# Two decoder layers on one core: half of the state products moved to the mixer's norm, the gate's 16 columns computed in fp32, the last norm done by tokens

## The reference

```python
def rms_norm(x, g):
    return x * lax.rsqrt(jnp.mean(x * x, axis=-1, keepdims=True) + EPS) * g

def half_ffn(x, g_pre, g_post, w_gate, w_up, w_down):      # D=1024, F=2816
    h = rms_norm(x, g_pre)
    f = (jax.nn.silu(h @ w_gate) * (h @ w_up)) @ w_down
    return x + 0.5 * rms_norm(f, g_post)

def mixer(h, ...):
    z = h @ w_in            # gq gk gv gg | glr: 16 columns | sq sk sv | conv
    log_a = log_sigmoid(glr @ gla_w_a2 + gla_b_a) / GLA_TAU
    # gated linear attention: per head, S_new = exp(b_last) * S + (k * exp(b_last - b))^T v
    # stick-breaking attention over 2048 cached positions, causal conv of 31 taps
    return concat(groups) @ w_out, k_new, v_new, s_new, buf_new

def decoder_layer(x, ...):
    x = half_ffn(x, ...)                                   # FFN 1
    x = x + rms_norm(mixer(rms_norm(x, mix_norm_pre)), mix_norm_post)
    return half_ffn(x, ...)                                # FFN 2
```

## Time and profile before

| | |
|---|---|
| runs of the kernel (median of 3; lowest, highest) | 1443.51 us; 1441.48, 1445.41 |
| the profiled execution | 1444.73 us, of which the trace's span is 1443.1 us |
| PE busy | 1405.8 us (97%) |
| DVE, ACT, POOL busy | 899.5 us (62%), 738.4 us (51%), 179.6 us (12%) |
| HBM read and written | 242.91 MB, 5.53 MB |
| mean granted TensorE clock | 0.99 of full speed |

### The profile page before, as it was taken

How to read it: one execution, slowest core, us unless ns; L and a number is a source line. 1 busy time by engine, 2 the same in 40 slices (tenths; PEclk the granted TensorE clock), 3 DMA queues, 4 the chain that set the end, 5 groups by cost and what they waited for, 6 DMA issues and landing times.

```text
span 1443.1 us, 26817 instructions
## 1 busy us (share of the span) xinstructions
PE 1405.8 (97%) x10515; PEld 1329.7 (92%) x10515; DVE 899.5 (62%) x1496; ACT 738.4 (51%) x1198; POOL 179.6 (12%) x326
## 2 busy tenths in 40 slices
PE   7999999999999999999999999999999999999997
PEld 6999999988877899999999999999887689999996
DVE  5665633679985766653367655355899747766542
ACT  4544433588855544343364444355886555443431
POOL 0020000323254000000000000021423510000000
PEclk9999999999999999999999999999999999999998
DMA  9565555567798575545545555556867894554441
GB/s 239 147 204 150 145 150 156 163 199 223 212 294 270 149 189 153 146 139 156 156 130 151 146 146 146 146 153 176 249 201 232 270 250 130 150 154 146 147 135 37
DMA packets 391362, 250.23 MB, mean 173 GB/s; under 512 B 14369, under 2 KB 379446, under 8 KB 391236
## 3 DMA queue, kind: packets, MB, share of 16 engines
q1 hardware_dynamic: 375602, 205.86, 50.0%
q0 software_dynamic: 15328, 42.52, 9.5%
q10 hardware_dynamic: 306, 0.13, 0.0%
HBM read 242.91 MB, written 5.53 MB: 172 GB/s over the span
## 4 chain that ended last, share of the span: by engine, by line
PE 89%; DVE 5%; ACT 3%; DMA 2%; issue 1%; SPq 0%; ACTq 0%
PE bank L571 23%; PE bank L572 23%; PE bank L573 23%; PE bank L772 3%; PE bank L882 2%; PE bank L607 2%; PE bank L611 2%; PE bank L608 2%; DVE fT L1619 2%; PE bank L787 2%; PE bank L943 1%; PE bank L737 1%; DVE w_l L1470 1%; DMA raw<-in_ffn_w_up 1%; DMA raw<-in_ffn_w_gate 1%
## 5 line engine op out<-in xcount | busy, mean ns | idle before, releaser
L1470 DVE TENSOR_TENSOR w_l<-raw,w_h 128x1024 fp32r<-128x1024 f32 (+1 forms) x334 | 397.6, 1197 | 301.7 <-ACT w_h L1119 301.7
L571 PE MATMUL bank<-hh,w_h 128*128 128x320 f32 x1648 | 517.5, 314 | 0.0
L573 PE MATMUL bank<-hh,w_l 128*128 128x320 f32 x1648 | 509.2, 309 | 0.0
L572 PE MATMUL bank<-hl,w_h 128*128 128x320 f32 x1648 | 509.1, 309 | 0.0
L1119 ACT ACTIVATE w_h<-raw 128x1024 fp32r<-128x1024 f32 (+1 forms) x334 | 334.6, 1030 | 144.2 <-DMA raw<-in_ffn_w_down 98.8
L571 PEld LDWEIGHTS bank<-hh,w_h 128*128 128x128 f32 x1648 | 309.4, 188 | 11.4 <-issue 8.6
L572 PEld LDWEIGHTS bank<-hl,w_h 128*128 128x128 f32 x1648 | 309.6, 188 | 0.5
L573 PEld LDWEIGHTS bank<-hh,w_l 128*128 128x128 f32 x1648 | 309.4, 188 | 0.0
L573 PE MATMUL bank<-guh,w_l 128*128 128x320 f32 x704 | 217.4, 309 | 0.0
L571 PE MATMUL bank<-guh,w_h 128*128 128x320 f32 x704 | 217.4, 309 | 0.0
L572 PE MATMUL bank<-gul,w_h 128*128 128x320 f32 x704 | 217.4, 309 | 0.0
(11 more groups left out here) (268 smaller groups left out, 1601.7 us busy)
## 6 DMA issues: line engine op xcount, KB each, us to landing
raw<-in_ffn_w_gate SPq DMA_DIRECT2D x88, 512.0 KB, 3.9
raw<-in_ffn_w_up SPq DMA_DIRECT2D x88, 512.0 KB, 3.9
raw<-in_ffn_w_down SPq DMA_DIRECT2D x64, 448.0 KB, 3.7
raw<-in_w_in SPq DMA_DIRECT2D x46, 512.0 KB, 4.1
raw<-in_ffn_w_down SPq DMA_DIRECT2D x32, 512.0 KB, 4.0
kpg<-in_cache_sb_k SPq DMA_DIRECT2D x112, 128.0 KB, 3.1
kpg<-in_cache_sb_k POOLq DMA_DIRECT2D x112, 128.0 KB, 2.6
raw<-in_w_out SPq DMA_DIRECT2D x16, 512.0 KB, 8.1
```

The lines of the kernel that those rows point to most:

```text
L571: pe.matmul(out, w_h[:, slot, k, :], rhs_h[:, k0 + k, :], start=first, stop=False)
L572: pe.matmul(out, w_h[:, slot, k, :], rhs_l[:, k0 + k, :], start=False, stop=False)
L573: last = pe.matmul(out, w_l[:, slot, k, :], rhs_h[:, k0 + k, :], start=False, stop=end)
L1470: V(dve.tensor_tensor(w_l[:, slot, 0:n, :], raw[:, slot, 0:n, :], w_h[:, slot, 0:n, :].bitcast(F32), ALU.subtract), sm["w_lo"])
```

## The change

Three parts, in one step.

1. Of the state products of each layer, those of sequences 0 to 3 stay where they were; those of 4 to 7 are issued after the mixer's `post_mean`. DVE's eight instructions for them go between the second and the third `lo` at the entry of FFN 2. `out_part` no longer waits for these (it waits for the first eight, and for `o_r`). POOL's store of the states waits for them, under a semaphore of its own (`st_out`); `st` and `aend` lie elsewhere in SBUF, and DVE waits for `st_out` before it writes there in FFN 2.
2. The gate's 16 columns are loaded alone (64 KB instead of 512 KB), not split by ACT; DVE clears 128x256 and multiplies them by the norm's gains. PE makes 8 fp32 matmuls of 128x32 weights on `xT` itself, the eight tiles in four column groups. The groups are added by the next product: `gla_w_a2` stands four times, at partitions 0, 32, 64 and 96 of `wa2_all`, and `log_gates` contracts over 128 rows.
3. In the last FFN the output tiles alternate between banks 0 and 1, and `last_down` turns them (scaled by the gains) to tokens two at a time while the next units run; DVE copies them to `yt`. The means are six narrow products with tokens as rows (`ss` and `sq` as weights), and after the last unit `xT` is turned as well. ACT makes `rsT` for 3 columns, and six DVE instructions scale, add and write the output rows.

```diff
@@ unit of the gate: SP, DVE, PE @@
+                    sp_.dma_start(raw[:, SLOT[u], 0, :].rearrange("p (k r) -> p k r", r=16), ins["w_in"][l, :, c:c + 16].rearrange("(k p) r -> p k r", p=P)).then_inc(w_loaded[SLOT[u]], 16)
...
+                    V(dve.memset(raw[:, slot, 2:4, :], 0.0))
+                    V.settle()
...
+                    V(dve.tensor_tensor(out, w, par_all[:, l, 8:16].unsqueeze(2).to_broadcast([P, KD, 16]), ALU.mult), sm["w_lo"])
+                    return
...
+                def gate_rows(u, out, part):
+
+                    pe.wait_ge(sm["w_lo"], u + 1)
+                    w = raw[:, SLOT[u], 2:4, :].rearrange("p a c -> p (a c)").rearrange("p (k r) -> p k r", r=32)
+                    for k in part:
+                        g = k % 4
+                        last = pe.matmul(out[32 * g:32 * g + 32, :], w[:, k, :], xT[:, k, :], start=(k < 4), stop=(k >= 4), skip_group_check=True)
+                    if k == KD - 1:
+                        last.then_inc(sm["w_used"], 1)
...
-                    if h == last_h:
+                    if m == M_LR:
+                        gate_rows(u, out, range(4))
+                    elif h == last_h:
                         unit(u, out, hh, hl, part=range(4))
...
-                        V(dve.tensor_tensor(glr[:, :], in_bank(m)[0:16, 0:T], rs[0:16, :], ALU.mult), sm["zin_dve"])
+                        V(dve.tensor_tensor(glr[:, :], b_, rs[:, :], ALU.mult), sm["zin_dve"])
@@ state products: PE @@
                 pe.wait_ge(*at("knm_ready", 1))
-                for b in range(DB):
...
+                state_products(0)
+                pe.wait_ge(*at("conv_d", 2))
+                state_products(1)
...
-                pe.wait_ge(*at("st_done", 16))
+                pe.wait_ge(*at("st_done", 8))
+                pe.wait_ge(*at("o_r", 4))
                 out_part(0, 2)
...
                 post_mean(M1)
+                pe.wait_ge(sm["f_ready"], 8 * M1 + 3)
+                state_products(2)
+                state_products(3)
                 ffn(2 * l + 1, 3 * l + 2, U + U_FFN2)
@@ state products: DVE, POOL @@
                 for q in range(4 if M % 3 == 2 else 5, 8):
                     lo(u0 + q)
+                    if M % 3 == 2 and q == 5:
+                        new_states(M // 3, (2, 3))
...
-                    pool.dma_start(outs["sample_gla_state"][l, :, 2 * p_:2 * p_ + 2].rearrange("b h k v -> (h k) b v"), st[:, :, p_, :]).then_inc(so, 16)
+                    pool.dma_start(outs["sample_gla_state"][l, :, 2 * p_:2 * p_ + 2].rearrange("b h k v -> (h k) b v"), st[:, :, p_, :]).then_inc(sm["st_out"], 16)
@@ the last FFN: PE @@
+            def last_down(g0, M, Ud):
+
+                for n in range(KD):
...
+                    for m, (k0, kn_) in enumerate(DOWN):
...
+                        unit(Ud + 3 * n + m, bank[n % 2][:, 0:T], guh, gul, k0, FT)
+                        if m == 0 and n in (2, 4, 6, 7):
+                            pe.wait_ge(sm["f_ready"], 8 * M + n)
+                        if m == 0 and n in (2, 4, 6):
...
+                            turn_outputs((n - 2, n - 1), ((a_, 0), (a_, 256), (b_, 0)))
+                        if m == 0 and n == 7:
+                            pe.wait_ge(sm["yf_placed"], 4)
+                            turn_outputs((6,), ((bank[4], 0), (bank[4], P), (bank[4], 2 * P)))
+                            pe.wait_ge(sm["ss_done"], 6 * M + 6)
+                            for t in range(NT):
+                                pe.matmul(bank[5][:, t:t + 1], ss[:, TOK[t]:TOK[t] + P], cst_("mean_d", cols=1), start=(t == 0), stop=False, skip_group_check=True)
+                turn_residual(0, (bank[6], bank[7]))
+                pe.wait_ge(sm["fsq_ready"], 8 * M + 8)
+                for t in range(NT):
+                    last = pe.matmul(bank[5][:, t:t + 1], sq[:, 1, TOK[t]:TOK[t] + P], cst_("mean_d", cols=1), start=False, stop=True, skip_group_check=True)
+                last.then_inc(sm["y_mean"], 1)
+                pe.wait_ge(sm["f_ready"], 8 * M + 8)
+                pe.wait_ge(sm["yf_placed"], 8)
+                turn_outputs((7,), ((bank[4], 0), (bank[4], P), (bank[4], 2 * P)))
+                turn_residual(1, (bank[2], bank[3]))
+                turn_residual(2, (bank[0], bank[1]))
@@ the last FFN: DVE @@
+            dve.wait_ge(sm["y_r"], 1)
+            for g in range(2):
...
+                    V(dve.scalar_tensor_tensor(yt[rows, t, c], yt[rows, t, c], rsT[rows, t:t + 1], b_[rows, :], ALU.mult, ALU.add), sm["y_placed"])
```

More of the change, by code:

```diff
@@ L54 @@
 NIN = len(UNITS_IN)
+M_LR = 8
 U_FFN = 2 * FT + 3 * KD
@@ L201, in settle, with splits @@
         self.eng.wait_ge(*self.last)
+def splits(u):
+    return u + 1 - sum(u >= l * U_END + U_IN + M_LR for l in range(L))
 def tiles_of(u):
@@ L623, in post_mean, with turn_outputs, turn_residual @@
                 pe.matmul(bank[0][:, 0:T], cst_("mean_d"), sq[:, 1, :], start=False, stop=True).then_inc(sm["post_mean"], 1)
+            def turn_outputs(tiles, places):
+                for i, n in enumerate(tiles):
+                    for t, (b_, c0) in enumerate(places):
+                        last = pe.transpose(b_[:, c0 + i * P:c0 + (i + 1) * P], fT[:, n, TOK[t]:TOK[t] + P], cst_("ident"))
+                last.then_inc(sm["yf_turned"], 1)
+            def turn_residual(t, banks):
+                for g, b_ in enumerate(banks):
+                    for j in range(4):
+                        last = pe.transpose(b_[:, j * P:(j + 1) * P], xT[:, 4 * g + j, TOK[t]:TOK[t] + P], cst_("ident"))
+                    last.then_inc(sm["yx_turned"], 1)
@@ L937, in _ @@
                         turn_weights(m - 20)
-                    unit(u, out, hh, hl, part=range(4, KD) if h == last_h else range(7, KD))
+                    if m == M_LR:
+                        gate_rows(u, out, range(4, KD))
+                    else:
+                        unit(u, out, hh, hl, part=range(4, KD) if h == last_h else range(7, KD))
                 def gla_outputs(pair):
@@ L1095, in _ @@
                     turn_keys_early(1, 0, (1, 2, 3, 0), 2)
-            for g in range(2):
-                pe.wait_ge(sm["x_ready"], 8 * (3 * L - 1) + 4 * g + 4)
-                for n in range(NT):
-                    rows = P if n < 2 else TS
-                    for j in range(4):
-                        last = pe.transpose(bank[2 + 2 * n + g][0:rows, j * P:(j + 1) * P], xT[:, 4 * g + j, n * P:n * P + rows], cst_("ident"))
-                    last.then_inc(sm["y_turned"], 1)
         @block.scalar
@@ L1453, in _ @@
                 ffn(2 * l + 1, 3 * l + 2, U + U_FFN2)
-            for n in range(NT):
-                rows = P if n < 2 else TS
-                act.wait_ge(sm["y_turned"], n + 1)
-                A(nsa(xn[0:rows, n, 0:512], bank[2 + 2 * n][0:rows, :], ACT.Copy), sm["y_placed"])
+            act.wait_ge(sm["y_mean"], 1)
+            rsqrt(bank[5][:, 0:NT], rsT[:, :], rln[:, 0:NT], sm["y_r"])
+            act.wait_ge(sm["yf_turned"], 5)
+            A(nsa(yt[:, 0:2, 7 * P:], bank[4][:, 0:2 * P].rearrange("p (t c) -> p t c", t=2), ACT.Copy), sm["y7_placed"])
+            A(nsa(yt[TS:P, 2, 7 * P:], bank[4][TS:P, 2 * P:3 * P], ACT.Copy), sm["y7_placed"])
         @block.vector
@@ L1516, in post_norm, with new_states @@
                     h_lo(N + 1, KD - 1)
+            def new_states(l, pairs):
+                for pair in pairs:
+                    dve.wait_ge(sm["st_prod"], l * per["st_prod"] + pair + 1)
+                    for b in (2 * pair, 2 * pair + 1):
+                        for p_ in range(2):
+                            c0 = (b % 2) * 256 + p_ * DV
+                            V(dve.scalar_tensor_tensor(st[:, b, p_, :], st[:, b, p_, :], aend[:, p_, 2 + b:3 + b], bank[S_BANK[pair]][:, c0:c0 + DV], ALU.mult, ALU.add), sm["st_done"])
             def settle_in(M, u0):
@@ L1551, in ffn @@
                         dve.wait_ge(sm["gu_hi"], g0 + 2 * i + t + 1)
+                        if k2 % 2 and i == 5 and t == 0:
+                            dve.wait_ge(sm["st_out"], (k2 + 1) // 2 * per["st_out"])
                         V(dve.tensor_tensor(gul[:, 2 * i + t, :], gt[:, t, :], guh[:, 2 * i + t, :].bitcast(F32), ALU.subtract), sm["gu_lo"])
@@ L1842, in _ @@
                 mix_lo(0, 2)
-                for b in range(DB):
-                    if b % 2 == 0:
-                        dve.wait_ge(*at("st_prod", b // 2 + 1))
-                    for p_ in range(2):
-                        c0 = (b % 2) * 256 + p_ * DV
-                        V(dve.scalar_tensor_tensor(st[:, b, p_, :], st[:, b, p_, :], aend[:, p_, 2 + b:3 + b], bank[S_BANK[b // 2]][:, c0:c0 + DV], ALU.mult, ALU.add), sm["st_done"])
+                new_states(l, (0, 1))
                 gla_read((2, 3))
@@ L1877 @@
 O_BANK = (6, 4)
-S_BANK = (2, 3, 0, 1)
+S_BANK = (2, 3, 1, 2)
 def head(h):
```

121 lines of the change are left out of this document (84 added, 37 removed).

## The result

The changed kernel takes 1431.34 us (median of 6 runs, 1427.58 to 1434.57) where the kernel before takes 1443.87 us on the same chip (6 runs, 1441.48 to 1445.41): a ratio of 0.9919, 95% interval 0.9906 to 0.9932. In a second series it took 1428.19 us (4 runs, ratio 0.9887, 0.9868 to 0.9906); the two intervals only touch, at 0.9906, so together they put the gain between 10 and 19 us. The ten runs together have a median of 1430.2. The prediction was 1429.5, in a range of 1425.5 to 1435.

A forecast was written before the change was run, and what follows sets the result against it. TensorE, busy 1405.8 of 1443.1 us, was taken as the bound. Terms -6.65 (part 1), -4.2 (part 2) and -3.9 (part 3) sum to -14.75 on 1444.73, giving 1430.0, carried as 1429.5 us; range 1425.5 to 1435.

The forecast's parts named there:

- Part 1, out of the mixer: Mixer: half the state products leave a stretch where TensorE is the bound, -1.83 us per layer, -3.65 in all.
- charge of 0 for the next group of values: Mixer, after the shortened state products: values still arrive in time, cost 0, at worst 1 us per layer.
- Part 1, the clock at the norm: Layer 1's mixer norm: with the gap filled the clock's fall goes away, -2.5 us, bounds 0 and -2.5.
- Part 1, ScalarE's late square: Layer 1's mixer norm: loads of `kpz` moved later, so ScalarE's weight split no longer waits for its transfer, -0.5 us.
- Part 2: Gate's unit in the mixer: 16 narrow fp32 records replace 24 matmuls, -2.1 us per layer, -4.2 in all.
- `log_gates` has the same count of columns over 128 rows instead of 16: 0: Small product behind the gate's unit: contracting over more rows costs or saves nothing.
- 0.2 held back for ScalarE: Gate's unit: -2.3 us per layer cut to -2.1 because ScalarE, losing only one split, may follow late.
- rival of VectorE as the mixer's bound: Mixer: only what VectorE itself sheds counts, 0.7 us per layer instead of 2.1; total 1432.3 us, chance 0.06.
- Part 3: Program's end: 3.65 us added before the last unit's end, 9.4 after it, against 16.96: -3.9 us.
- the clock gives it back: Rival: clock falls at layer 1's norm (+2.5) or the end (+3.1), or values late (+1 per layer); two give 1434.5; chance 0.18.
- "slower" rival: Thinner stretches between 405 and 460 us let the clock fall at each; eight falls give 1448 us; chance 0.04.
- no overlap: Gate's unit: four column groups don't overlap, 5.6 us, +2.1 instead of -2.1 per layer; total 1437.9 us, chance 0.07.

The follow-up runs named there:

- part 1 alone: Kernel before with only the state products of sequences 4 to 7 moved to the mixer's norm, with the stores this needs: 1440.14 us against 1443.33, ratio 0.9972.
- changed again: The changed kernel run once more, unchanged, as base of the second series: 1428.19 us, ratio 0.9887 to the kernel before.
- one group: Changed kernel with the gate's eight fp32 products all in the first 32-column group instead of four groups: 1435.18 us, ratio 0.9946 to the kernel before.
- filler: Kernel before plus 16 unused state products behind the norm's means in each layer, nothing moved out of the mixer: 1441.11 us, ratio 0.9988.
- part 2 alone: Kernel before with only the gate's 16 columns as fp32 products in four column groups, and their preparation: 1437.45 us, ratio 0.9953.
- part 3: Kernel before with only the last norm done by tokens: 1436.67 us, ratio 0.9955.
- early turns: Changed kernel with weight turn 5 ahead of the remaining state products, turns 6 and 7 into the output products: 1425.23 us, ratio 0.9875 to the kernel before.

## Why the prediction was right, and where it was not

**Part 1, out of the mixer: -3.65.** The rest falls by 2.0 us in layer 1 and, with the 0.7 put back, by about 1.7 in layer 2: -3.7 in all. The step holds for TensorE. What failed is the charge of 0 for the next group of values, which the prediction worked out from layer 1 alone: of the four profiles with part 1, whole transfers and nothing moved further, three show the seventh group in layer 2 late, by 1.75, 1.81 and 1.19 us (part 1 alone, changed again, one group). Less the 0.69 us that TensorE waited there before, it costs 1.1, 1.1 and 0.5 us, about the 1 us put down as the worst for a layer.

**Part 1, the clock at the norm: -2.5.** That filling the gap gains time is shown by the filler. That it stops the fall each time, as the step has it, is not so, and its size was read from one execution. In the kernels without products in the gap (before, part 2, part 3) 3 of 6 gaps of the mixer's norm were followed by a fall, at 2.5, 1.6 and 1.2 us. With them, 4 of 22, at 1.4 us each. Per execution of two layers that is 1.8 against 0.5, so the filling is worth an estimated 1.3 us, and the filler measured 1.8 (0.3 to 3.2). The prediction set a fall that comes half of the time at its full price, and the chance of one afterwards at zero.

At the end of the program the clock was 1.00 over the whole of the new tail's transposes (first row below, of the changed kernel), and the end was 9.3 us in all nine profiles that have part 3. The Trainium skill's page TensorE: Matmul & The Clock Gate, Part 4, has transposes not count as activity. The trace differs where the clock is at its upper level: it stayed there while they ran, and the measurement decides. The old tail is on the page's side: there the clock had fallen while TensorE idled, and it stayed at 0.50 under all 24 transposes (second row, of the kernel before).

```profile
1416.00:1420.50 4.50, 4.36 (x39) 1.00 0.02 6
```

```profile
1435.00:1440.00 5.00, 3.47 (x16) 0.50 0.51 169
```

**Part 1, ScalarE's late square: -0.5.** The wait in front of the norm's second mean appears in layer 1 of two of the four kernels that keep the loads of `kpz` at the norm (0.57 in before, 0.87 with part 2), and in none of the ten that load them later. The cause fits; the size per execution is 0.4.

**Part 2: -4.2.** The 16 records took 1.33 instead of 1.25 us, so -2.21 per layer instead of -2.3. One column group gave 4.52, near the 5.6 of the rival, and so the overlap of the four groups is shown. The step that failed is "`log_gates` has the same count of columns over 128 rows instead of 16: 0": it is -0.39 per layer, shown by the rows of part 2 alone. The Trainium skill's page TensorEngine Tiling (Array Packing), Key Properties, says that a change of tiling mode drains TensorE. With 16 rows these products lie between full-height ones, and with 128 rows no such change is left, so the trace agrees with that rule here, where the prediction had looked for it at the unit only; no run shows that this is the cause. And the 0.2 held back for ScalarE was not needed: the rest of both layers falls by 2.8 and 2.5, -5.3 in all. The rival of VectorE as the mixer's bound (0.7 per layer) is refuted by this.

**Part 3: -3.9.** Before the last unit's end it added 3.0 us instead of 3.65, after it 9.3 stand instead of 9.4: -4.7. The terms of the 3.65 were each too large, most of all the four changes of shape at 0.11: three transposes took 0.33 and six narrow records 0.59 with the way back to the unit, so 21 transposes and the six make 2.9 and leave 0.1 for the changes that were to cost 0.45.

**The clock, elsewhere.** The rival "the clock gives it back" is partly what happened, at another place than it named. Low clock cost 3.4 us per execution in the mixers of before, filler, part 2 and part 3 (5.1, 3.5, 3.4, 1.7), and 6.5 in the five with part 1 and nothing further (8.5, 5.1, 6.8, 6.9, 5.1). That is +3 us, from few executions with a wide spread, so a tendency and not shown. With it the sum comes near the runs: -8.7 in the mixers' rest (part 1 and part 2 together, changed and changed again), -1.3 and -0.4 at the norm, -4.7 at the end, +3 for the clock and +0.6 for the seventh group make about -11.5, and the two series measured -11.7 and -16.3 by their ratios. The second lies 5 us beyond it, and no profile shows why. The three parts measured alone (-4.0, -6.8 and -6.5) make -17.3, near the second series and 5.6 more than the first; whether they cost each other something when put together, the runs do not settle.

So it is in part luck that the total came out right. Terms that were too small (part 2 by 1.1, part 3 by 0.8) stood against a clock gain at the norm that was too large by about 1.2, a late group of values, and a loss to the clock in the mixer that the main case had at nothing. The eight falls of the "slower" rival did not come; nor did "no overlap".

**What stays open.** What makes the clock fall in the mixer. It is not the idle in front of the sample's products alone: without it the low stretches stayed, and with 1.6 us of it (part 3 and one group, both in layer 1) there were none. And whether the version with early turns is faster than the changed kernel: 1425.23 against 1428.19 us beside it, with intervals that overlap. All kernels that go further end between 0.9875 and 0.9892 of the kernel before. Their profiles have new waits for the values' transfers in the place of those they saved on ScalarE and VectorE; that this is what holds them together is likely and not shown.

## What to carry to other kernels

Before a stall is counted as a loss of the clock, look at the same place in other layers and executions, and take the price times how often it falls; a filler that computes nothing tests it in one run. When work is taken out of a full TensorE stretch that eats transfers, put the transfers' own pace beside it first, in each layer: here one group was late as soon as 2 us were gone. Spread a narrow product over many rows over the four column groups, and let the small product behind it add the groups over 128 rows.

## What the runs showed of the hardware beyond what was expected

- Four fp32 records over 16 rows and 320 columns took 1.27 us from start to next start, over 128 rows 0.84 us, and 2.49 against 2.10 us with the rows on both sides: more rows in the contraction made it faster.
- In two pieces, 16 records of 128x32 fp32 weights and 320 columns took 1.33 us over four column groups and 4.52 us in one: a factor of 3.4.
- A gap of 2.9 us with 1.96 us of small 64x64 products in it can still be followed by a fall of the clock (4 of 22 times, at 1.4 us each). With 2.8 us of idle in the gap there was a fall 3 of 6 times, at 1.2 to 2.5 us.
- The low stretches in the mixers were 3.4 us long (1.7 us lost) or 6.8 us (3.4 lost); their number differed between two executions of the same program.
- A clock at 1.00 stayed there through 27 transposes in the 3.7 us after the last unit; a clock at 0.50 stayed there through 24 transposes in two pieces of 2.82 us.
